# Hybrid three-mixer trunk: first loads split and regrouped, first tiles reordered, last residual tiles loaded ahead

## What is computed

```python
for l in range(DEPTH):
    h = rmsnorm(x, pre_norm[l])
    proj = jnp.einsum('bld,de->ble', h, w_in[l])       # 6,680 columns
    ... = split_cols(proj, IN_SIZES)
    o_a = gated_deltanet(...)                          # 4 heads, chunk-causal
    y_b = ssd(...)                                     # 16 heads in 2 groups
    o_c = retention(...)                               # 4 heads, rotary q and k
    mixed = concat(norm(o_a)*silu(gz), norm(y_b*silu(sz)), norm(o_c)*silu(rg))
    out = jnp.einsum('ble,ed->bld', mixed, w_out[l])
    x = x + rmsnorm(out, post_norm[l])
```

## Time and profile before

| What | Value |
|---|---|
| Median of 3 runs | 2396.87 us (2395.07 to 2397.87) |
| Profiled execution, its own time | 2396.32 us |
| Its span, from first to last instruction | 2394.5 us |
| PE busy | 2313.7 us (97%) |
| DVE, ACT, POOL busy | 1303.8, 761.9, 503.8 us |
| DMA | 339.27 MB, mean 142 GB/s |
| Mean granted TensorE clock | 0.996 |

### The profile page before, as it was taken

One profiled execution on the slowest core, in us unless ns is written; L12 is line 12 of the kernel. 1 busy time (PEld: TensorE's weight loads), 2 busy tenths in 40 slices (PEclk: granted clock), 3 DMA queues, 4 the chain that ended last, 5 costly groups with the idle time before them and its releaser, 6 DMA issues. The chain is left out here.

```text
span 2394.5 us, 37085 instructions
## 1 busy us (share of the span) xinstructions
PE 2313.7 (97%) x15032; PEld 2044.7 (85%) x15032; DVE 1303.8 (54%) x2284; ACT 761.9 (32%) x1373; POOL 503.8 (21%) x448
## 2 busy tenths in 40 slices
PE   5999999999999999999999999999999999999995
PEld 4887888998888889899888898889988889889995
DVE  3766578435556565624555756853445554573233
ACT  3644344232423234112444423422233323331000
POOL 2443333330100011101243323423211000110000
PEclk9999999999999999999999999999999999999998
DMA  5644422555323324343544442545632232343412
GB/s 190 230 159 158 159 106 97 190 207 195 122 86 100 116 88 151 131 144 123 203 173 167 167 154 93 184 142 197 237 130 93 93 115 80 129 153 98 158 54 97
DMA packets 78649, 339.27 MB, mean 142 GB/s; under 512 B 8976, under 2 KB 9744, under 8 KB 65040
## 3 DMA queue, kind: packets, MB, share of 16 engines
q1 hardware_dynamic: 77760, 335.45, 41.0%
q10 hardware_dynamic: 720, 1.45, 0.2%
HBM read 219.42 MB, written 117.44 MB: 141 GB/s over the span
## 5 line engine op out<-in xcount | busy, mean ns | idle before, releaser
L1024 PE MATMUL ps<-w_hi,hT_hi 128*128 128x256 f32 x1792 | 526.2, 294 | 1.6 <-POOL w_low L1958 1.6
L1024 PE MATMUL ps<-w_low,hT_hi 128*128 128x256 f32 x1792 | 504.6, 282 | 0.0
L1024 PE MATMUL ps<-w_hi,hT_lo 128*128 128x256 f32 x1792 | 499.8, 279 | 0.0
L1024 PE MATMUL ps<-wo_loaded,mixT 128*128 128x256 f32 x2048 | 457.7, 379 | 3.5 <-DVE et L1592 3.4
L1024 PEld LDWEIGHTS ps<-wo_loaded,mixT 128*128 128x128 f32 x2048 | 384.0, 190 | 60.1 <-issue 5.8
L1958 POOL TENSOR_TENSOR w_low<-w_loaded,w_hi 128x512 fp32r<-128x512 f32 x208 | 284.4, 1384 | 449.1 <-ACT w_hi L1718 449.0
L1024 PEld LDWEIGHTS ps<-wk 128*128 128x128 f32 x2336 | 294.9, 191 | 92.4 <-DVE wk L1479 30.2
L1024 PE MATMUL ps<-wk 128*128 128x128 f32 (+2 forms) x2336 | 343.3, 286 | 11.4 <-DVE wk L1502 1.8
L1024 PEld LDWEIGHTS ps<-w_low,hT_hi 128*128 128x128 f32 x1792 | 340.3, 190 | 1.3 <-issue 0.2
L1024 PEld LDWEIGHTS ps<-w_hi,hT_hi 128*128 128x128 f32 x1792 | 337.0, 188 | 3.8 <-POOL w_low L1958 2.3
L1024 PEld LDWEIGHTS ps<-w_hi,hT_lo 128*128 128x128 f32 x1792 | 339.3, 189 | 0.0
(11 more groups left out here) (178 smaller groups left out, 2721.1 us busy)
## 6 DMA issues: line engine op xcount, KB each, us to landing
w_loaded<-in_w_in SPq DMA_DIRECT2D x104, 512.0 KB, 5.1
w_split<-w_hi SPq DMA_DIRECT2D x52, 1024.0 KB, 8.1
w_split<-w_low SPq DMA_DIRECT2D x52, 1024.0 KB, 10.1
w_hi<-w_split SPq DMA_DIRECT2D x104, 512.0 KB, 5.5
w_low<-w_split SPq DMA_DIRECT2D x104, 512.0 KB, 6.6
wo_loaded<-in_w_out SPq DMA_DIRECT2D x64, 512.0 KB, 3.6
wk<-in_x SPq DMA_DIRECT2D x8, 512.0 KB, 6.4
xfin<-in_x SPq DMA_DIRECT2D x8, 512.0 KB, 5.2
```

The lines of the kernel that those rows point to most:

```text
L1024: return nc.tensor.matmul(o, a, b, start=start, stop=stop)
```

## The change

Six edits belong together:
- The constants are laid out anew, so that what the first steps need (`C_ID` to `C_ZERO`, 532 columns) comes first. ACT loads these 532 columns, `par` of layer 0 and both `row` tables; SP loads the other 1924 columns and `par` of layer 1 later (semaphore `later`). TensorE and POOL wait for the first load alone; DVE waits for the first two loads and the row tables too, but only behind its two memsets.
- All four x tiles of part 0 load at once: tiles 2 and 3 go to another place in `wk` (`x_tile`).
- In the plan, `rescale` and `norm` of tiles 0 and 1 come before the weight splits, and `norm` of tiles 2 and 3 after slices 4 and 8 of the first piece.
- The slices of the first piece wait for their own tile, in all four parts.
- The exponential of `A_log` and its negation (`nega`) are made at the step where they are first needed.
- In the last part the four old x tiles are loaded into `wk` after the last retention output (`x_last`, semaphores `last_in`), and the last additions wait for these.

Its core (shifted waits of POOL and the planner's costs are left out):

```diff
--- before.py
+++ after.py
@@ -149,12 +149,12 @@
 
     add(("scale", 0, 0))
     add(("scale", 0, 1))
-    for j in range(4):
-        add(("split", 0, 0, j))
-    for t in range(NT):
+    for t in range(2):
         add(("norm", 0, t), ("rescale", 0, t))
-        if t < 2:
-            add(("scale", 0, t + 2))
+    for t in range(2, NT):
+        for j in range(2 * t - 4, 2 * t - 2):
+            add(("split", 0, 0, j))
+        add(("scale", 0, t))
     for p in range(PARTS):
         for i, piece in enumerate(PIECES):
             for half in range(2):
@@ -176,6 +176,8 @@
                     add(("proj", p, i, half, q), *needs)
                     if last and q in (3, Q - 1):
                         add(("scale", p + 1, 2 + (q > 3)))
+                    if not p and (i, half) == (0, 0) and q in (3, 7):
+                        add(("norm", 0, 2 + q // 4), ("rescale", 0, 2 + q // 4))
                     if p and (i, half, q) == (0, 0, 1):
                         add(("norm", p, 3), ("rescale", p, 3))
                     if (i, half, q) == (0, 1, 3):
@@ -805,6 +813,8 @@
         rqT, rkT, rqd, rS, rkd = (flat[:, i * 512:(i + 1) * 512].rearrange("p (c n) -> p c n", c=NT) for i in range(5))
 
         xin = flat[:, 3584:3584 + 2 * D].rearrange("p (a b) -> p a b", a=2)
+        x_tile = lambda n: flat[:, (n - 2) * D:(n - 1) * D] if n in (2, 3) else xin[:, n % 2, :]
+        x_last = lambda t: flat[:, t * D:(t + 1) * D]
         sm_t = flat[:, 3584 + 2 * D:3584 + 2 * D + 6 * NT * NDEC].rearrange("p (a b) -> p a b", a=6)
 
         smT = flat[0:NSM, 2560:3072]
@@ -891,27 +903,29 @@
 
         unit_use = lambda u: u if u[0] == "small" else (*u, NT // 2 - 1)
         for n, u in enumerate(units):
-            loads.append((where[unit_use(units[n - 2])] if n >= 2 else -1, n, u))
+            loads.append((where[unit_use(units[n - 2])] if n >= 2 else -3 if u[0] == "small" else -1, n, u))
         for n in range(PARTS * len(PIECES)):
             p, i = divmod(n, len(PIECES))
             release = ("proj", *divmod(n - W_RING, len(PIECES)), 1, Q - 1)
-            loads.append((where[release] if n >= W_RING else -2, n, ("in", p, i)))
+            loads.append((where[release] if n >= W_RING else -5 if n == 0 else -2, n, ("in", p, i)))
             if p % 2 == 0:
                 loads.append((where["proj", p, i, 0, Q - 1], n, ("keep", p, i)))
         for n in range(PARTS * NT):
             p, t = divmod(n, NT)
-            release = [where["norm", (n - 2) // NT, (n - 2) % NT]] if n >= 2 else [-3]
+            release = [where["norm", (n - 2) // NT, (n - 2) % NT]] if n >= NT else [-6 if n < 2 else -4]
             if p and t < 2:
                 release.append(where["ssd_y", p - 1, SG - 1, NT - 1])
             if p >= 2:
                 release.append(where["final", p - 2, t])
             loads.append((max(release), n, ("x", p, t)))
 
-            loads.append((where["final", p, t - 1] if t else where["mix_turn", p, 2], n, ("rest", p, t)))
+            loads.append((where["ret_o", p, RH - 1, NT - 1] if p == PARTS - 1 else where["final", p, t - 1] if t else where["mix_turn", p, 2],
+                          n, ("rest", p, t)))
             loads.append((where["final", p, t], -1, ("store", p, t)))
         for p in range(PARTS):
             loads.append((where["mix_turn", p, 2], p, ("post", p)))
             loads.append((where["gdn_decay", p, 0], p, ("rope", p)))
+        loads.append((-3, PARTS, ("later", 0)))
         loads.sort()
         block = ctx.enter_context(nc.Block())
 
@@ -945,14 +959,21 @@
         def _(sp):
             for _, n, key in loads:
                 kind, p = key[:2]
-                if kind == "x":
-                    if n >= 2:
+                if kind == "later":
+                    sp.dma_start(con[:, C_LEV:], cons[:, C_LEV:]).then_inc(later, 16)
+                    for l in range(1, DEPTH):
+                        sp.dma_start(par[:, l, :], pars[l]).then_inc(later, 16)
+                elif kind == "x":
+                    if n >= NT:
                         wait_filled(sp, ("norm", (n - 2) // NT, (n - 2) % NT, 1))
                     if p and key[2] < 2:
                         wait_filled(sp, ("ssd_y", p - 1, SG - 1, NT - 1, "w"))
                     if p >= 2:
                         sp.wait_ge(x_stored[key[2]], 16 * (p - 1))
-                    sp.dma_start(xin[:, n % 2, :], x_rows(p, key[2])).then_inc(x_in[n % 2], 16)
+                    sp.dma_start(x_tile(n), x_rows(p, key[2])).then_inc(x_in[n if n < 4 else n % 2], 16)
+                elif kind == "rest" and p == PARTS - 1:
+                    wait_filled(sp, ("ret_o", p, RH - 1, NT - 1))
+                    sp.dma_start(x_last(key[2]), x_rows(p, key[2])).then_inc(last_in[key[2]], 16)
                 elif kind == "rest":
                     if key[2]:
                         sp.wait_ge(S["f_done"], n)
@@ -1036,7 +1057,7 @@
                         tag = (*s, j)
                         b = opened(tag)
                         for c in range(4):
-                            i = turn(b[:, c * P:(c + 1) * P], xin[:, (NT * p + t) % 2, (4 * j + c) * P:(4 * j + c + 1) * P])
+                            i = turn(b[:, c * P:(c + 1) * P], x_tile(NT * p + t)[:, (4 * j + c) * P:(4 * j + c + 1) * P])
                         close(i, tag)
                 elif k == "small":
                     b = opened(s)[0:NSM, :]
@@ -1068,8 +1089,8 @@
                     tag = s[:4]
                     if q == 0:
                         opened(tag)
-                        if i_ == 0:
-                            wait_emptied(pe, ("norm", p, 2 * half + 1, 1))
+                    if i_ == 0 and 2 * q % KD == 0:
+                        wait_emptied(pe, ("norm", p, 2 * half + 2 * q // KD, 1))
                     b = bank(tag)
                     wide = PIECES[i_][0] in ("gdn", "bc", "sx")
                     v, k0 = divmod(2 * q, KD)
@@ -1323,11 +1344,10 @@
                 tt(L3, L3, over_rows(gT[:, c, :], HG), ALU.mult).then_inc(S["ssd_lg"], 1)
 
             conv_at = None
-            dve.wait_ge(loaded, 16 * (1 + 2 * DEPTH))
             chain(nc.vector.memset(sm_t[:].rearrange("p a b -> p (a b)"), 0.0))
             clear_states()
-            dve.wait_ge(S["nega_ready"], 1)
-            chain(ts(nega[:], nega[:], -1.0, None, ALU.mult))
+            dve.wait_ge(loaded, 16)
+            dve.wait_ge(pars_in, 16 * (1 + DEPTH))
             for s in plan:
                 k, p = s[0], s[1]
                 l, first_half = p // 2, p % 2 == 0
@@ -1449,6 +1472,8 @@
                     h = s[2]
                     n = GH * p + h
                     own = sc[:, n % 2]
+                    if n == 0:
+                        dve.wait_ge(later, 16 * DEPTH)
                     dve.wait_ge(S["gdn_et"], n + 1)
                     tag = (*s, 0)
                     wait_filled(dve, tag)
@@ -1659,8 +1684,11 @@
                     dve.wait_ge(S["f_rstd"], n + 1)
                     dve.wait_ge(post_in, 16 * (p + 1))
                     chain(stt(acc[:, t, :], acc[:, t, :], frs[:, t:t + 1], post[:], ALU.mult, ALU.mult))
-                    dve.wait_ge(xf_in, 16 * (n + 1))
-                    tt(acc[:, t, :], acc[:, t, :], xfin[:], ALU.add).then_inc(S["f_done"], 1)
+                    if p < PARTS - 1:
+                        dve.wait_ge(xf_in, 16 * (n + 1))
+                    else:
+                        dve.wait_ge(last_in[t], 16)
+                    tt(acc[:, t, :], acc[:, t, :], xfin[:] if p < PARTS - 1 else x_last(t), ALU.add).then_inc(S["f_done"], 1)
 
         @block.scalar
         def _(act):
@@ -1680,26 +1708,28 @@
                     act.wait_ge(*junk_read.pop())
                 junk_read.append(read_by)
 
-            act.dma_start(con[:], cons).then_inc(loaded, 16)
+            act.dma_start(con[:, 0:C_LEV], cons[:, 0:C_LEV]).then_inc(loaded, 16)
+            act.dma_start(par[:, 0, :], pars[0]).then_inc(pars_in, 16)
             for l in range(DEPTH):
-                act.dma_start(par[:, l, :], pars[l]).then_inc(loaded, 16)
-                act.dma_start(row[:, l, :], rows[l].partition_broadcast(P)).then_inc(loaded, 16)
-            act.wait_ge(loaded, 16 * (1 + 2 * DEPTH))
-            A(nega[:], row[:, :, R_A:R_A + NDEC], ACT.Exp).then_inc(S["nega_ready"], 1)
+                act.dma_start(row[:, l, :], rows[l].partition_broadcast(P)).then_inc(pars_in, 16)
             for s in plan:
                 k, p = s[0], s[1]
                 l, first_half = p // 2, p % 2 == 0
                 if k == "scale":
                     t = s[2]
                     n = NT * p + t
-                    act.wait_ge(x_in[n % 2], 16 * (n // 2 + 1))
+                    act.wait_ge(x_in[n if n < 4 else n % 2], 16 * max(n // 2, 1))
                     square_into_junk((S["x_squares"], n + 1))
```

(8 more changed lines are left out.)

41 lines of the change are left out of this document (28 added, 13 removed).

## The result

| | Before | Changed |
|---|---|---|
| Median of 4 runs | 2396.25 us (2395.07 to 2397.87) | 2371.93 us (2370.63 to 2372.61) |
| Profiled execution, its span | 2396.32, 2394.5 us | 2371.52, 2369.7 us |
| Mean granted TensorE clock | 0.996 | 0.996 |

The ratio is 0.9897, with a 95% interval of 0.988 to 0.9915. The change saves 24.3 us; 28.5 were predicted, and the time lies within the range.

What follows compares the result with a forecast made beforehand. TensorE itself bounds the main stretch; gains lie before its first matmul, between its first two blocks and behind its last. Front 18.4 plus end 10.1 gives 28.5 us off the 2396.87 median: 2368.4, range 2365.5 to 2373.5.

Steps and rivals of the forecast that it cites:

- Half rate in the first slices: Front: TensorE partly at half rate in its first slices, 0.9 us added, between full-rate end 28.1 and half-rate end 31.2.
- Rival 1: Front: tile 0 lands no earlier than 7.5, all moves by 2.4 us, time 2370.8; chance 0.08.
- The signs: Trace marks of right (first transpose 9 to 10, first slice 14 to 15, small matmuls 28 to 31) or wrong.
- Rival 2: Front: TensorE stays at half rate through the first slices, piece ends at 31.2, time 2370.6; chance 0.10.
- Rival 3: Front: piece 0's weight write-back comes 5 us late and returns part of the gain, time 2373.4; chance 0.05.
- The 0.8 us that the range gives to a still earlier tile 0: Range's lower side: tile 0 landing at 4.3 instead of 5.1 would give 0.8 us more gain.
- Now two follow: 9.6-2.4+3.8 = 11.0: Front: two small row loads follow the first parameters at 1.9 us each, so VectorE can start at 11.0.
- the tiles and weights are there: five more big loads take 5 to 7 us: Front: five big loads behind tile 0 at 416 GB/s take 5 to 7 us, so ScalarE never waits.
- the likeliest case: Whole run: the forecast itself, gain 28.5 us, median 2368.4, small matmuls from 29.0; chance 0.72.
- The shift should reach the end: Middle: order on all engines stays as before, so the front's 18.4 us gain arrives whole, 0 lost.
- rival 4: Beyond the first piece: TensorE keeps the lower clock; 57 us of it lose all 28.5 us, then slower; chance 0.01.
- The hidden terms: End: early x loads delay a weight load under cover, 0 (else to 2 us); POOL powers beside DVE, 0.5 (0 to 1.8).

Runs made afterwards that it cites:

- second profile: The changed kernel unaltered, profiled once more in one execution: span 2369.1 us, small matmuls from 32.56 us, middle 2322.89 us.
- second profile of before: The kernel before, unaltered, profiled once more: 2396.23 us, span 2394.4 us, middle 2323.41 us, end 23.17 us.
- experiment 2: Kernel before with only the end changed (the last part's four old x tiles loaded ahead): 2386.22 us, ratio 0.9955 to the kernel before.
- experiment 3: Changed kernel with the old loads and last additions of the end put back, front alone: 2383.52 us, ratio 0.9941 without one outlier.
- experiment 4: Changed kernel with all constants in the first load again (1228 KB): 2373.7 us, ratio 0.9901 to the kernel before.
- experiment 6: Changed kernel plus 18 unused identity transposes behind tile 1's, filling TensorE's pause: 2371.49 us, ratio 0.9887 to the kernel before.
- experiment 5: Changed kernel with layer 0's parameters on their own semaphore, so VectorE's first split skips the row tables: 2369.52 us, ratio 0.9882 to the kernel before.
- experiment 10: Changed kernel with layer 0's parameters awaited separately, six filler transposes, and all four weight splits before tiles 2 and 3's Squares: 2369.65 us, ratio 0.9882.
- experiment 7: Changed kernel with the transposes of tiles 2 and 3 ahead of the first slice again, early loads kept: 2374.04 us, ratio 0.9897 to the kernel before.
- experiment 11: The changed kernel unaltered, a third time, on another chip: 2372.04 us, ratio 0.9894 to the kernel before there.
- experiment 9: Changed kernel with layer 0's parameters awaited apart from the row tables, plus six filler identity transposes: 2367.88 us, ratio 0.9879 to the kernel before.
- experiment 8: Changed kernel with ScalarE's old order, weight splits ahead of the rescales of tiles 0 and 1: 2373.78 us, ratio 0.9899 to the kernel before.

## Why the prediction was right, and where its sum was off

The steps, each against its measurement, in us:

| Step of the prediction | Predicted | Measured |
|---|---|---|
| Tile 0 lands | 5.1 | 5.4 |
| Row tables landed, VectorE starts | 11.0 | 12.38 |
| Tile 2 lands | in time for 11.5 | 13.3 |
| First slice | 14.5 | 16.05 |
| Half rate in the first slices | +0.9 | +1.7 (second profile +3) |
| Small matmuls begin | 29.1 | 31.27 (second profile 32.56) |
| Middle | 0 | -1.9 (second profile 0) |
| End, gain | 10.1 | 10.5 (9.5 against the second profile of before) |
| Whole gain | 28.5 | 24.8 (medians 24.3, and 25.6 on another chip) |

**Mechanism.** Front and end are what was gained, in the proportion predicted, and they add (experiments 2 and 3). The landing of tile 0 went by the row-by-row reading of the two landings in the earlier trace rows; experiment 4 puts both back at once, tile 0 at 7.5 and the constants at 8.0. Rival 1 is out by that.

**The signs.** Not all of them came as the prediction named them. The first transpose (9.30), the additions without a wait for a DMA and 2.45 us apart, and the early landing of tile 0 did. But the first slice (16.05, not 14 to 15) and the small matmuls (31.27, not 28 to 31) lie outside their ranges, and "matmuls of the first slices 0.2 us apart", a sign of being wrong, is what happened: 0.21. The time falls within the stated range, in which rivals 1 to 3 had a place too; the forecast itself, 2368.4, was 3.5 us too low. The 0.8 us that the range gives to a still earlier tile 0 is more than the sum's own terms allow, since there the row loads hold VectorE to 11.0 whenever tile 0 lands.

**The row tables and tile 2 (about 1.4 us).** "Now two follow: 9.6-2.4+3.8 = 11.0" was too small by 1.4. The par load landed as reckoned (7.4 against 9.6-2.4 = 7.2), but the two row loads behind it, 28 KB each, took until 12.3, 4.9 us for the two instead of 3.8. And "the tiles and weights are there: five more big loads take 5 to 7 us" was wrong for tile 2: issued at 2.79, it landed 10.5 us later. The sum counted the bytes from tile 0 on, but tile 2 is the fifth of the big loads on its queue, and they share the way with the constants. That this alone makes it so late is not shown. At full rate the front would have stood at 28.2 by the sum; with the pause filled it stands at 29.61 (experiment 6). Tile 2's delay costs nearly that much by itself: with the row tables out of the way and the clock up, the front still stands at 29.45, since GpSimd's subtractions then hold it (experiment 5). What the row tables' delay alone would cost at full rate, no run shows.

**The clock in the first slices (0.8 us in the first profile).** The term was seen, but only a part of it was taken, and the pause behind the transposes was reckoned as 1.2 us. It was 3.4, because VectorE was late. A late table thus costs twice, once as a wait and once as the clock. Rival 2, half rate through all four slices, is what the second profile shows, at 32.56 even beyond its 31.2, since the late rows come on top. So the likeliest case and rival 2 are one kernel in different executions.

**The middle (1.9 us).** "The shift should reach the end" failed as a step in the first profile: the order of work did reach the end, but TensorE's clock fell near 194 us. Of the fourteen profiled executions here, three have the old start (before, before again, the end alone) and none of these has a fall in the middle. Of the eleven with the new start seven have one or two, always near one of three places: 188 to 202 (the changed kernel twice, experiments 5 and 10), 872 to 884 (experiments 3, 7 and 11), 2036 to 2044 (experiments 6 and 10). At 187 to 194 us TensorE waits several times for 0.2 to 0.5 us; ahead of 872 to 877 and of 2036 us it waits once for 1.0 us, for VectorE. These waits are there in the executions without a fall, too. Each fall costs 1 to 2 us; the middles without one lie between 2322.86 and 2323.41 us.

None out of three against seven out of eleven points to the new start, but the three are few, and the executions without a trace show that they aren't typical. Each of these has a mean granted clock on record. For the kernel before it is 0.996 in both profiles, where the clock is low only behind the last matmul; at half for the whole 24.0 us behind that matmul it would be 0.995. Of the 22 other executions of that kernel with a recorded clock, 14 have 0.992 to 0.994, so their clock was low somewhere ahead of that, too. Of the end alone one execution has 0.995, where the profiled one has 0.998, and took 2389.14 us, 2.8 more. No trace says where. It can have been in the middle, or in the pause of 8.26 us between the two blocks of transposes, where a low clock costs little. So it stays open whether the new start makes falls in the middle likelier, and the 1.9 us can't be booked to the change: two executions without a fall in the middle, before (span 2394.5) and the second profile of the changed kernel (2369.1), lie 25.4 us apart. If the new start does cost it, that is rival 4's mechanism (a loss by the lower clock) at a fifteenth of its fatal size. No experiment filled these pauses.

**Rival 3** is out. Piece 0's write-back was issued at 17.87 and 18.24 us and landed after 5.9 and 7.9, by 26.1, 5 us before it is wanted; TensorE's list of waits names no DMA. **The hidden terms** held: the four early loads of old x tiles are issued at 2309.41, land after 5.3 us in the median, and no gap of TensorE follows. GpSimd's two powers beside VectorE took 1.47 us each, but VectorE's pairs stayed 2.45 apart, so neither the 0.5 us taken for them nor the 2.6 us worked out from the shared port was lost.

**What each part of the front is worth**, by the experiments: the order on ScalarE 1.9 to 3.2 us, the short constants load 1.7 to 3, the slices moved forward 1.1 to 2.4. Each was priced with the other two in place, and in executions whose own first slices ran in part at half rate. The rest, by subtraction 7.6 us of the first profile's 16.2 or 10.2 of the second's 14.9, would be the start without waiting for all five loads and the four tiles loaded at once; this was only argued, no run took that part alone.

## What to carry to other kernels

At the start of a kernel each first instruction should wait for exactly the loads that it reads: here tables of 28 KB that nobody needed yet cost 1.8 to 3.1 us of front (experiment 5), as much as the megabyte of constants (1.7 to 3 us, experiment 4), because they came last in their queue and their delay made a pause in which TensorE stood at or fell to the lower clock. When the sum of a front is made, look at when the last loads in each queue land. Where TensorE would pause before its first dense work, a few transposes of the identity can be cheaper than the pause (experiment 6; with a pause of 1.25 us and the clock already up, six of them gained 0.2 us). And where a change of 1 us matters, read the granted clock of the middle in more than one execution, of both kernels, before the difference is given to the change.

## What was not expected of the hardware

- At the start of the program the granted clock column reads 1.00 while sixteen transposes take 3.65 us, against 1.91 for sixteen late ones. In the second profile it reads 1.00 until 22 us, through slices at half rate. The trace has no clock record for these stretches: its first one starts at 36.0 us in the kernel before, at 12.2 and 22.0 in the two profiles of the changed kernel and at 23.9 in experiment 7, each time where the spacing of the matmuls goes from half to full rate. Ahead of the first record only that spacing (0.21 or 0.12 us) tells the level.
- The same instructions with the same pauses at 187 to 194 us ran once at a granted clock of 1.00 (experiment 9) and once fell to 0.50 (the changed kernel).
- The pause alone does not decide: after 1.25 us the first slice went at full rate in experiment 5 and at half rate in experiment 8 (first matmul 0.38 and 0.58 us). In experiment 5 the clock had come up at 12.6 us, as the transposes ended; in experiment 8 it came up only at 22.9, so in both the slices began at the level that stood ahead of the pause.
- One execution of experiment 3 took 4671.81 us, about twice the others' time, with a recorded clock of 1.0; no trace of it exists, and its cause is open.
